# A two-layer diffusion backbone: the opening reordered, the projection's modulation started at its head, one group of modulation pieces moved into the MLP

## The reference

```
cond_x = silu(c);  cond_c = silu(c_ctx)
for i in range(2):
    mx = split(cond_x @ ada_w[i] + ada_b[i], 6)      # shift, scale, gate for the mixer, the same for the MLP
    mc = split(cond_c @ ada_w[i] + ada_b[i], 6)
    hx = rms_norm(x, g[0]) * (1 + mx[1]) + mx[0]      # context in the same way with mc
    ox, oc = attention_mixer(hx, hc, ...)             # i == 0; long convolution and SSD where i == 1
    x = x + mx[2] * rms_norm(ox, g[1])
    x = x + mx[5] * rms_norm(sq_relu_mlp(rms_norm(x, g[2]) * (1 + mx[4]) + mx[3], ff_w1[i], ff_w2[i]), g[3])
```

## Time and profile before

| | us |
|---|---|
| Median of three runs | 3417.53 |
| The profiled execution's own time | 3420.0 |
| Its span | 3418.1 |
| PE busy | 3287.9 (96%) |
| DVE busy | 1894.7 (55%) |
| ACT busy | 1284.3 (38%) |
| Start of the projection stage | 73.4 |

### The profile page before, as it was taken

The page is one execution under the profiler, slowest core; times in us unless marked ns, Lnnn a source line. Parts: engine busy times, 40 slices in busy tenths (PEclk is TensorE's granted clock), DMA queues, the critical chain, the costliest instruction groups (busy, mean ns, idle before and its releaser), DMA issues. The chain is left out here.

```text
span 3418.1 us, 39368 instructions
## 1 busy us (share of the span) xinstructions
PE 3287.9 (96%) x15248; PEld 2427.2 (71%) x15248; DVE 1894.7 (55%) x2428; ACT 1284.3 (38%) x2110; POOL 699.5 (20%) x383
## 2 busy tenths in 40 slices
PE   6999999999999999999999999889999999999998
PEld 3665445555888888888899878653457788888886
DVE  3334444433757665674686534577685654445444
ACT  4333444445543323433454222552113542333222
POOL 0000787665341001300230100110012410002001
PEclk8999999999999999999999999999999999999999
DMA  5636333321554454543465311103413433333333
GB/s 224 231 103 207 91 66 78 85 55 42 169 175 128 145 162 145 167 152 97 155 215 161 107 44 39 45 38 114 176 33 116 138 127 96 95 97 126 116 93 105
DMA packets 146650, 406.64 MB, mean 119 GB/s; under 512 B 25497, under 2 KB 39609, under 8 KB 143648
## 3 DMA queue, kind: packets, MB, share of 16 engines
q1 hardware_dynamic: 146464, 404.11, 36.9%
HBM read 345.05 MB, written 58.92 MB: 118 GB/s over the span
## 5 line engine op out<-in xcount | busy, mean ns | idle before, releaser
L1737 PE MATMUL psum<-h_high,w_high_and_low 128*128 128x512 f32 (+1 forms) x1536 | 415.7, 356 | 0.0
L1754 PE MATMUL psum<-hid_high,w_high_and_low 128*128 128x512 f32 (+1 forms) x1536 | 413.7, 355 | 1.7 <-DVE hid_low L2003 1.5
L2025 POOL TENSOR_TENSOR squares_then_rstd_of_out<-squares_then_rstd_of_out,square_out 128x512 f32<-128x512 f32 (+1 forms) x69 | 105.5, 1529 | 1264.9 <-ACT square_out L1824 1264.9
L1415 POOL TENSOR_TENSOR probs_added<-probs_added,probs_turned 128x1024 f32<-128x1024 f32 x128 | 308.2, 2407 | 66.4 <-ACT probs_turned L1340 53.8
L1382 DVE TENSOR_REDUCE row_max<-psum 128x1 f32<-128x1280 f32 x120 | 179.0, 1492 | 228.6 <-PE psum L1278 137.1
L1809 ACT ACTIVATE w_high_and_low<-w_raw 128x1024 fp32r<-128x1024 f32 x192 | 202.4, 1054 | 270.9 <-PE psum L1754 244.6
L1737 PEld LDWEIGHTS psum<-h_high,w_high_and_low 128*128 128x128 f32 x1536 | 272.8, 189 | 43.7 <-issue 3.7
L1754 PEld LDWEIGHTS psum<-hid_high,w_high_and_low 128*128 128x128 f32 x1536 | 272.8, 189 | 43.2 <-DVE hid_low L2003 2.3
L2000 DVE TENSOR_TENSOR hid_high<-hid_relu_and_square 128x512 fp32r<-128x512 f32 (+1 forms) x160 | 111.2, 695 | 326.0 <-ACT hid_relu_and_square L1894 325.5
L1737 PE MATMUL psum<-h_low,w_high_and_low 128*128 128x512 f32 (+1 forms) x768 | 271.7, 354 | 0.0
L1754 PE MATMUL psum<-hid_low,w_high_and_low 128*128 128x512 f32 (+1 forms) x768 | 271.7, 354 | 0.0
(11 more groups left out here) (492 smaller groups left out, 6790.5 us busy)
## 6 DMA issues: line engine op xcount, KB each, us to landing
w_raw<-in_ff_w_dram SPq DMA_DIRECT2D x292, 512.0 KB, 3.5
ada_ring<-in_ada_w_dram SPq DMA_DIRECT2D x12, 2048.0 KB, 14.7
ada_rows_in<-in_ada_w_dram SPq DMA_DIRECT2D x96, 256.0 KB, 3.6
w_raw<-in_w_out_dram SPq DMA_DIRECT2D x38, 512.0 KB, 3.5
ada_rows_added<-in_ff_w_dram SPq DMA_DIRECT2D x28, 512.0 KB, 3.8
scratch_spectra<-spectrum_out SPq DMA_DIRECT2D x32, 256.0 KB, 2.0
filter_ring<-scratch_spectra SPq DMA_DIRECT2D x16, 512.0 KB, 3.9
stream_in<-scratch_x SPq DMA_DIRECT2D x27, 256.0 KB, 4.3
```

Source lines behind the costliest of these rows:

```text
L1415: pool.tensor_tensor(total, old, pt[:, i % RING, :, 0:nq], ALU.add).then_inc(added, 1)
L1737: mm = pe.matmul(bank[:, 0:n], x[i % SLOTS][:, k, :], y[:, k, a:a + n], start=(k == 0 and m == 0), stop=(k == KT - 1 and m == 2))
L1754: mm = pe.matmul(bank[:, 0:n], x[i % SLOTS][:, 2 * k + half, :], y[:, k, 0:n], start=(k == 0 and m == 0), stop=(k == HT - 1 and m == 2))
L2025: pool.tensor_tensor(acc_out[:, q % 2, 0:n], acc_out[:, q % 2, 0:n], sq_out[:, v % 2, 0:n], ALU.add).then_inc(added_out, 1)
```

## The change

- The opening keeps one `Modulation` object for the opening and the projection, with order 2, 3, 0, 1, then 4 to 9. Its weights of pieces 4, 5 and 6 are asked for at the end of the opening, as are three of the four tables; the sine table is loaded first in the projection, and only DVE waits for it.
- The two first weight tiles are loaded before the tokens of chunk 1, and rounded before chunk 1 is squared.
- The ring for squares has 4 places instead of 8. The 8 squares of chunk 1 are added by DVE (7 additions), and PE makes one matmul of the sum. It stands behind the multiply of the third piece.
- ACT copies piece 3 between `shift(0, FRONT)` and `shift(1, FRONT)`; DVE takes all low parts after the fourth bias.
- In the projection, pieces 4 to 9 are multiplied at steps 0, 1, 2, 5, 7 and 9, and turned a step later.
- Pieces 10 and 11 of layer 0 (both streams) become batch 0 in the MLP; the old batches move one place back, and the last one stands at steps 126 to 145.

```diff
-ADA_LATER = [(0, piece) for piece in range(4, ADA_PIECES)]
-ADA_IN_MLP = [(1, (2, 3), BOTH), (1, (0, 1), BOTH)] + [(1, (4, 5, 6, 7), LATENT), (1, (8, 9, 10, 11), LATENT)]
+ADA_LATER = [(0, piece) for piece in range(4, 10)]
+ADA_IN_MLP = [(0, (10, 11), BOTH), (1, (2, 3), BOTH), (1, (0, 1), BOTH)] + [(1, (4, 5, 6, 7), LATENT), (1, (8, 9, 10, 11), LATENT)]
...
-    SUMS, RING = (3, 4, 5), KT
+    SUMS, RING = (3, 4, 5), 4
...
                 ada.load(sp, 1)
+                for t in range(2):
+                    sp.dma_start(g.first_raw[:, t], d["w_qk"][t]).then_inc(w_first, 16)
                 load_x(1)
                 ada.load(sp, 2)
-                for t in range(2):
-                    sp.dma_start(g.first_raw[:, t], d["w_qk"][t]).then_inc(w_first, 16)
                 ada.load(sp, 3)
                 load_x(2)
+                for dst, src in ((g.by_head, "by_head"), (g.swap, "swap_a"), (g.cos_a, "cos_a")):
+                    sp.dma_start(dst[:], d[src]).then_inc(g.tabs_in, 16)
+                for i in range(NEEDED, NEEDED + ada.SLOTS):
+                    ada.load(sp, i)
...
+                    if c == 1:
+                        pe.wait_ge(added, KT - 1)
+                        pe.matmul(g.ps[:, SUMS[c], 0:n], g.ones[:], sq_sum[:, 0:n], start=True, stop=True).then_inc(used, 1)
+                        return
...
                 for i in range(NEEDED):
+                    ada.multiply(pe, i)
                     if i == 2:
                         add_squares(1)
-                    ada.multiply(pe, i)
                     ada.turn(pe, i)
...
                 ada.copy(act, 1)
-                of_x(1)
-                root(1)
-                ada.copy(act, 2)
-                act.wait_ge(ada.biased, 3)
-                shift(0, FRONT)
-                shift(1, FRONT)
                 act.wait_ge(w_first, 32)
                 for t in range(2):
                     act.activation(g.first_high[:, t], g.first_raw[:, t], ACT.Copy).then_inc(w_rounded, 1)
+                of_x(1)
+                ada.copy(act, 2)
+                root(1)
+                act.wait_ge(ada.biased, 3)
+                shift(0, FRONT)
                 ada.copy(act, 3)
+                shift(1, FRONT)
...
                 scale(0, BACK)
-                scale(1, range(KT))
-                ada.bias(dve, 2)
-                split_off(0, FRONT)
-                split_off(1, FRONT)
+                for k in range(1, KT):
+                    dve.wait_ge(squared, KT + k + 1)
+                    if k > 1:
+                        dve.wait_ge(added, k - 1)
+                    dve.tensor_tensor(sq_sum[:], sq[:, KT % RING, :] if k == 1 else sq_sum[:], sq[:, (KT + k) % RING, :], ALU.add).then_inc(added, 1)
                 for t in range(2):
                     dve.wait_ge(w_rounded, t + 1)
                     dve.tensor_tensor(g.first_low[:, t], g.first_raw[:, t], g.first_high[:, t], ALU.subtract).then_inc(w_split, 1)
+                ada.bias(dve, 2)
+                scale(1, FRONT)
+                scale(1, BACK)
                 ada.bias(dve, 3)
-                split_off(0, BACK)
-                split_off(1, BACK)
+                for c in range(2):
+                    split_off(c, FRONT)
+                    split_off(c, BACK)
...
-    TILES, FIRST, ADA_FROM = 5, 3, 4
+    TILES, FIRST = 5, 3
+    ada_at = {step: len(ADA_FIRST) + m for m, step in enumerate((0, 1, 2, 5, 7, 9))}
...
-                ada.load_selector(sp)
-                for dst, src in ((by_head, "by_head"), (swap, "swap_a"), (cos, "cos_a"), (sin, "sin_a")):
-                    sp.dma_start(dst[:], d[src]).then_inc(tabs_in, 16)
+                sp.dma_start(sin[:], d["sin_a"]).then_inc(sine_in, 16)
                 ring.load(sp, 2, qk_piece(2))
-                for i in range(ada.SLOTS):
+                for i in range(len(ADA_FIRST) + ada.SLOTS, len(ada.order)):
                     ada.load(sp, i)
...
                     if step == 1:
-                        pe.wait_ge(tabs_in, 64)
+                        pe.wait_ge(tabs_in, 48)
...
-                    ada.turn(pe, step - ADA_FROM - 1)
-                    if step >= ADA_FROM:
-                        ada.multiply(pe, step - ADA_FROM)
+                    if step - 1 in ada_at:
+                        ada.turn(pe, ada_at[step - 1])
+                    if step in ada_at:
+                        ada.multiply(pe, ada_at[step])
...
-                dve.wait_ge(tabs_in, 64)
+                dve.wait_ge(tabs_in, 48)
+                dve.wait_ge(sine_in, 16)
```

More of the change, by code:

```diff
@@ L112, in __init__ @@
     def __init__(self, nc, g, d, mem, sems, pieces, banks):
-        self.g, self.w_in, self.order, self.banks = g, sems[:3], pieces, banks
+        self.g, self.w_in, self.order, self.banks, self.sems = g, sems[:3], pieces, banks, sems
         self.sel_in, self.made, self.copied, self.turned, self.biased, self.folded = sems[3:]
         self.w = tile(nc, mem, "ada_ring", [P, self.SLOTS, KT, BANK])
-        self.rows = tile(nc, mem, "ada_rows", [P, len(banks), BANK])
+        self.rows = tile(nc, mem, "ada_rows", [P, 2, BANK])
         self.sel = tile(nc, mem, "group_selector", [P, 2])
@@ L152, in copy @@
             act.wait_ge(self.turned, i - len(self.banks) + 1)
-        act.activation(self.rows[:, i % len(self.banks), :], self.bank(i), ACT.Copy).then_inc(self.copied, 1)
+        act.activation(self.rows[:, i % 2, :], self.bank(i), ACT.Copy).then_inc(self.copied, 1)
     def turn(self, pe, i):
@@ L161, in turn @@
         for m in range(BANK // P):
-            mm = pe.matmul(self.bank(i)[:, 2 * m:2 * m + 2], self.rows[:, i % len(self.banks), m * P:(m + 1) * P], self.sel[:], start=True, stop=True)
+            mm = pe.matmul(self.bank(i)[:, 2 * m:2 * m + 2], self.rows[:, i % 2, m * P:(m + 1) * P], self.sel[:], start=True, stop=True)
         mm.then_inc(self.turned, 1)
@@ L278, in opening @@
     FRONT, BACK = range(KT // 2), range(KT // 2, KT)
-    order = [(c, k) for tiles in (FRONT, BACK) for c in range(2) for k in tiles] + [(2, k) for k in range(KT)]
-    place = {x: m + 1 for m, x in enumerate(order)}
-    SUMS, RING = (3, 4, 5), KT
-    names = "cond_in ones_in vectors_in x_in0 x_in1 x_in2 cond_ready gain_ready squared used logged rstd scaled rounded split w_first w_rounded w_split"
-    names += " ada_in0 ada_in1 ada_in2 sel_in made copied turned biased folded"
+    rounded_by = {x: m + 1 for m, x in enumerate([(c, k) for tiles in (FRONT, BACK) for c in range(2) for k in tiles] + [(2, k) for k in range(KT)])}
+    split_by = {x: m + 1 for m, x in enumerate((c, k) for c in range(C) for k in range(KT))}
+    SUMS, RING = (3, 4, 5), 4
+    names = "cond_in ones_in vectors_in x_in0 x_in1 x_in2 cond_ready gain_ready squared used logged rstd scaled rounded split w_first w_rounded w_split added"
     with stage(nc, names) as (mem, sems):
@@ L286, in opening @@
         x_in = sems[3:6]
-        cond_ready, gain_ready, squared, used, logged, rstd, scaled, rounded, split, w_first, w_rounded, w_split = sems[6:18]
-        ada = Modulation(nc, g, d, mem, sems[18:], ADA_FIRST, (6, 7))
+        cond_ready, gain_ready, squared, used, logged, rstd, scaled, rounded, split, w_first, w_rounded, w_split, added = sems[6:19]
+        ada = g.ada
         x = tile(nc, mem, "x_then_scaled", [P, KT, TOK])
         sq = tile(nc, mem, "norm_square_x", [P, RING, BANK])
+        sq_sum = tile(nc, mem, "norm_squares_added", [P, BANK])
         rs = tile(nc, mem, "rstd_x", [P, TOK])
@@ L328, in first_unit @@
                     for k in range(KT):
-                        pe.wait_ge(split, place[c, k])
+                        pe.wait_ge(split, split_by[c, k])
                         for m, (w, y) in enumerate(((g.first_high, g.high), (g.first_high, g.low), (g.first_low, g.high))):
@@ L408, in split_off @@
                     for k in tiles:
[L409 removed]
+                        dve.wait_ge(rounded, rounded_by[c, k])
                         dve.scalar_tensor_tensor(out=g.low[:, k, a:a + n], in0=x[:, k, a:a + n], scalar=mod(SHIFT_A, k, c),
@@ L596, in _ @@
                 for step in range(U + 3):
-                    ada.copy(act, step - ADA_FROM - 1)
+                    if step - 1 in ada_at:
+                        ada.copy(act, ada_at[step - 1])
                     if step < U and step % C == 1:
@@ L3242, in build_program @@
         g.first_high, g.first_low = (tile_r(nc, g.first_ring, f"w_{x}", [P, 2, KT, P]) for x in ("high", "low"))
+        g.ada_memory = ExitStack()
+        g.by_head, g.swap = tile(nc, g.ada_memory, "ones_by_head", [P, P]), tile(nc, g.ada_memory, "swap_halves", [P, P])
+        g.cos_a, g.tabs_in = tile(nc, g.ada_memory, "cos_a", [P, TOK]), nc.alloc_semaphore("tables_in")
+        ada_sems = [nc.alloc_semaphore(n) for n in "ada_in0 ada_in1 ada_in2 sel_in made copied turned biased folded".split()]
+        g.ada = Modulation(nc, g, d, g.ada_memory, ada_sems, ADA_FIRST + ADA_LATER, (6, 7))
         opening(nc, g, d)
```

40 lines of the change are left out of this document (25 added, 15 removed).

## The result

The kernel after takes **3396.23 us** (median of 4 runs, 3393.08 to 3397.51), the kernel before beside it 3417.35 (4 runs, 3416.48 to 3422.53): ratio 0.9936, 95% interval 0.9924 to 0.9948.

The account below looks back on a forecast made before the run. PE was taken as the bound, at full clock outside the first slice. Pieces -16.0, head +4.6, opening -2.0, MLP +2.0 sum to -11.4 us: from the median 3417.5 to 3406.1, range 3398.5 to 3414.5 (8 in 10).

Parts of the forecast that it names:

- The projection's pieces: Projection body: fewer modulation pieces behind the first product, and no bias gap, cut 24.8 us to 8.8, saving 16.0.
- The rival in which ACT sets the pace: Projection, 92 to 173 us: PE may gain nothing if ACT's chain sets the pace; about 3418 us, chance 0.04.
- The projection's head: Start of projection: a chain through one PSUM bank replaces the sine-table wait; first product ends 4.6 us later than before.
- I expect half clock here: Projection's head: PE idle twice, about 3 us each, so half clock; multiply 3.8 us, clock back at 19.9 us.
- Rival 1: Head and opening: half clock costs little, so -20 us in all, 3398 us; chance 0.17.
- Rival 2: New chains are longer: head's first product 8 us late or more, opening gains nothing; -4 us, 3413.5; chance 0.22.
- The opening: Kernel's start: half clock from 28 us, yet first unit 2.4 us earlier; taken as -2.0 us, bounds -5 and +1.5.
- The rule weighed there: Opening: throttled clock is default, activity releases it, phase varies; taking PE work from a wait buys no time, costs clock.
- The MLP's own cost: MLP: PE is full, so the new batch's sum and turn are paid in full, +2.0 us, bounds +2 to +4.
- the slower rival: MLP steps 126 to 143: DVE becomes late and PE waits for low parts; +13 us, 3430; chance 0.05.
- The sign of being wrong: MLP: PE waiting for a low part there was named as one of the findings that would prove the forecast wrong.

Follow-up runs that it names:

- e1: Kernel before with only the third dt sum moved from PSUM bank 0 to bank 1: 3413.47 us, ratio 0.9986.
- e2: Kernel after with the third dt sum put back into PSUM bank 0: 3402.88 us, ratio 0.9956.
- e3: Kernel before with only pieces 10 and 11 of layer 0 moved into the MLP, dt sum kept in bank 0: 3411.24 us, ratio 0.9983.
- e4: Kernel after with the projection's six pieces at steps 4, 6, 8, 10, 12 and 14, none at its head: 3395.45 us, ratio 0.9933.
- e9: Kernel after with the two first weight tiles loaded behind chunk 1's tokens and rounded behind its squares: 3394.49 us, ratio 0.9932.
- e10: Kernel after with both the late weight tiles of e9 and the piece steps of e4: 3393.03 us, ratio 0.9928.
- e7: Kernel after with chunk 1's squares added by PE again, ahead of the third piece, without DVE's additions: 3400.63 us, ratio 0.9947.
- e12: Kernel after run again unchanged, beside the two combined edits: 3396.92 us, ratio 0.9939.
- e11: Kernel after with both the late weight tiles of e9 and the products one step ahead of e5: 3395.66 us, ratio 0.9933.
- e5: Kernel after with each of PE's products in the projection one step ahead of its place: 3396.04 us, ratio 0.9937.

## Why the prediction was wrong in size and right in sign

**The step that failed** is the MLP's: "PE is 110.0 of 110 us busy in the stretch where the new batch falls, so its sum and turn are paid in full", +2.0 us, and the sum then stops there. It counts what the new batch adds at its own place and doesn't ask what else is numbered by the list that the batch lengthens. The PSUM bank of the third dt sum is, and in before it was the one in which the next stage's first product starts, a wait of PE of 4.09 us. The move to bank 1 gave 5.4 us in the traces (e1 5.1, e2 5.4 in whole times). Without it the time would have been 3402 to 3403 (e2: 3402.88), inside the range and 3 to 4 us below the forecast. It is the largest part of what the sum lacks, not all of it. The traces differ by 22.4 us, 11.0 more than forecast: 5.4 are the bank, 3.7 the head, 2.9 the drain, 0.9 the opening, and the MLP and the rest take back some 2.

**The projection's pieces**, -16.0 forecast, -16.1 found. Counting periods of 3.16 in the earlier trace rows and taking out the gap was right in sum, though e3 found 6.9 for two periods of 6.3, and ACT and DVE kept up with the shorter steps. The rival in which ACT sets the pace is refuted.

**The projection's head**, +4.6 forecast, +0.9 found: the chain as forecast, one term mis-sized. "I expect half clock here" put multiply 5 at 3.8 us; it took 1.92, and the first turn and mean were at full clock too. The clock fell at about 80, 10 us after the stage's start, and cost only multiply 6 (3.64), turn 5 (1.73) and one mean (1.79). The product ended 20.4 us after the stage's start in place of 24.0. I had taken the clock of 73 to 82, where PE did nothing at all, for a stretch in which PE is busy 6.12 of 10 us, though the same rows gave no case between. Rival 1 (half clock costs little) was thus half right here. How near the +0.9 comes to the truth hangs on before's trace, though: against e1's trace of the same old head the new one costs 4.2 us, against e3's 2.3. One profile of before could not show that. That pieces at the head are paid is confirmed twice: three of them cost 9.8 us there against 7.9 in the body (after and e4), and 7.6 against 7.8 (e9 and e10). Rival 2, longer chains, is refuted: the product ended 3.6 us earlier than forecast, not later.

**The opening**, -2.0 forecast, -2.9 found. Transfers came as worked out (tokens 28.8 by 28.9, third piece 33.72 by 33.7), and so did half clock from 28 on. Not foreseen was full clock from 39 to 46: multiply 3 took 1.92, not 3.8, and the first unit began at 47.0, not 48.8. Half clock returned with the wait ahead of it, and 1.3 of the 4.2 us won at its start were lost by its end. Within the term two opposite things hid: DVE's additions gain (e7: 3.6 us in the gain over before, 1.7 at the first units' end), the early weights lose (e9: 2.5 us in the gain over before, 2.8 at the first units' end).

The rule weighed there, of the Trainium skill's page "TensorE: Matmul & The Clock Gate", section "Part 1: The HAM clock gate" (throttled is the default, activity releases it), had me expect that work taken from PE in a wait costs clock. e7 gives the work back, and this half of the rule agrees: with it PE has full clock from 36 to 46 us and 2.9 us less of half clock at the first units. But the price is larger than what it buys, since the work itself begins at half clock and stands ahead of the third piece (10.01 us). That taking it out "buys no time" is refuted. The other half of that rule, a phase that differs between runs, agrees as well. The two profiles of the kernel after (after and e12) have the first unit at 47.0 and 47.2, the key product at 170.3 and 170.7, but before and e1, the same program up to there, have the key product at 188.4 and 185.2, and e10's first units, with the opening of e9, end at 67.6, not 66.5.

**The MLP's own cost**, +2.0 forecast, +3.0 found. The new batch's sum and turn:

```profile
1612.00 1.06 PE L230 MATMUL psum<-ada_rows_added,all_ones 128*32 128x512 f32 x8
1618.58 0.95 PE L242 MATMUL psum<-identity,ada_sums 128*128 128x4 f32 x8
```

They are 2.0 us. Most of the rest is a wait of PE for the low part of a weight tile at the MLP's head, 1.27 us in after and 0.18 in before:

```profile
880.94 0.50 PE L1748 MATMUL psum<-h_high,w_high_and_low 128*128 128x512 f32 x1 [1.27 <-DVE w_high_and_low L1931]
```

That DVE becomes late in steps 126 to 143, the slower rival, is refuted: PE is busy all 140 us with DVE at 86. The sign of being wrong that goes with it, a PE that waits for a low part in the MLP, did come, at another place and for 1.1 us more than in before.

**The drain of the projection** was not in the sum: -2.9, of which 2.2 are the store's wait. e3 shows that it goes with the two pieces, not why. The last +1.4 us, behind the dt's turn, are within what one and the same stretch does from run to run (1386.1 us in before, 1387.5 in after and in e11, 1389.0 in e3): PE's busy time grows by the same 1.4, as it does when the clock falls otherwise. So are the 0.4 in the attention, which takes 623.7 us from fold to end in before, 623.2 in after and 624.5 in e4.

The range failed on the low side because it was built of the terms that I had. Its low end was rival 1 alone, and lay at 3398.5, above rival 1's own sum (3417.5 - 19.8 = 3397.7); no case in it held a gain at a place outside the change.

## What to carry to other kernels

When a change inserts or removes an entry of a list, search for everything that is computed from its length or index (banks, slots, due times), and check in the order of instructions who shares a bank with whom at the next stage's start. Positions of one and the same instruction in two traces, subtracted at eight or ten markers, find such a place at once, where shares of busy time don't. Bound a clock-dependent term by both levels and don't put it at the one that a neighbouring, emptier stretch shows. Profile the kernel before more than once: here two executions of one and the same head differ by 3 us. When two edits are tried together, compare the pair with each edit alone, not only with the kernel that neither changed.

## What the runs showed of the hardware

- A stretch with PE busy 6.12 of 10 us, in which it stood idle for up to 1.93 us at a time, kept its full clock (1.00) for about ten microseconds and then had 0.50 for six. In the earlier trace rows 2.97 us of work in 10 went with 0.50 throughout. The share of busy time doesn't give the clock: in the same window e5 is busy 7.98 us at 1.00, e10 8.19 us at 0.51.
- The same instructions have another clock in another execution: from 85 to 88 us 0.50 in before and 0.99 in e1.
- Eight sums of f32 squares over 128 partitions (16 recorded matmuls of 128x512) took 10.01 us, begun at half clock (e7), and 7.11 at full clock (before).
- A stage whose first product shares a PSUM bank with the stage before's last sums lost about 5 us here (e1 5.1, e2 5.4): PE waits 4.09 us for ACT's copy, 2.7 to 3.1 more than without, and the rest goes in matmuls at half clock behind it.
